# Two root-mean-square norms after the expert output: per-token sums in the expert stage, scaling, split, step-size product and store inside the second block's stage

## The reference, cut to what matters

```
x = x + mod[5][:, None, :] * peer(h, ...)        # first block, its end
x = rms_norm(x, final_g)                         # "final1": x * rsqrt(mean(x*x) + 1e-6) * final_g
h = rmsnorm(x, norm_w[l])                        # "norm_2", second block, its beginning
proj = h @ w_in[l]
a_q, a_f, a_i, a_z, b_x, b_z, c_z, c_xbc, c_dt, gate_logits = jnp.split(proj, split_idx, axis=-1)
...
x = x + jnp.sum(gates * branch_out, axis=2)      # the output of final1 is the residual
```

## Time and profile before

| | before |
|---|---|
| median of 3 runs | 4773.05 us |
| lowest and highest run | 4767.39, 4774.24 us |
| the profiled execution, its own time | 4772.02 us |
| its span | 4770.2 us |
| PE busy | 4418.3 us, 93% |
| DVE busy | 2832.7 us, 59% |
| ACT busy | 1814.2 us, 38% |
| POOL busy | 48.0 us, 1% |
| mean granted clock of PE | 0.965 |

### The profile page before, as it was taken

One profiled execution on the slowest core, in us unless ns is written; L12 is line 12 of the kernel. 1 busy time (PEld: TensorE's weight loads), 2 busy tenths in 40 slices (PEclk: granted clock), 3 DMA queues, 4 the chain that ended last, 5 costly groups with the idle time before them and its releaser, 6 DMA issues. The chain is left out here.

```text
span 4770.2 us, 76796 instructions
## 1 busy us (share of the span) xinstructions
PE 4418.3 (93%) x29238; PEld 3850.8 (81%) x29238; DVE 2832.7 (59%) x4753; ACT 1814.2 (38%) x2638; POOL 48.0 (1%) x63
## 2 busy tenths in 40 slices
PE   9798999897998995879999999999999599999996
PEld 1694444876998995879999999788888399999996
DVE  0448775665686446545776666455555556765645
ACT  0430000442653322334444555444444355444532
POOL 0000000000000000000000000000000000200000
PEclk9899999989999997989999999999999799999998
DMA  8357554326875331445665555666666255444452
GB/s 320 109 176 256 220 217 170 124 86 229 293 238 184 87 88 67 156 153 176 208 205 183 178 177 178 211 217 212 214 217 214 78 177 172 151 157 153 169 185 106
DMA packets 229517, 848.34 MB, mean 178 GB/s; under 512 B 86368, under 2 KB 124608, under 8 KB 139968
## 3 DMA queue, kind: packets, MB, share of 16 engines
q1 hardware_dynamic: 229312, 845.48, 52.0%
HBM read 794.95 MB, written 50.45 MB: 177 GB/s over the span
## 5 line engine op out<-in xcount | busy, mean ns | idle before, releaser
L282 DVE TENSOR_TENSOR rounded<-arena,rounded 128x1024 fp32r<-128x1024 f32 x464 | 567.7, 1225 | 647.1 <-ACT rounded L275 647.1
L275 ACT ACTIVATE rounded<-arena 128x1024 fp32r<-128x1024 f32 x464 | 490.6, 1059 | 787.0 <-PE bank L2340 391.3
L2018 PE MATMUL bank<-rounded,rounded 128*128 128x256 f32 x2048 | 590.8, 288 | 2.7 <-DVE rounded L2143 2.7
L2020 PE MATMUL bank<-rounded,rounded 128*128 128x256 f32 x2048 | 579.9, 283 | 0.0
L2019 PE MATMUL bank<-rounded,rounded 128*128 128x256 f32 x2048 | 579.7, 283 | 0.0
L351 PE MATMUL bank<-rounded,rounded 128*128 128x256 f32 x1664 | 479.1, 288 | 98.4 <-DVE rounded L282 98.4
L2701 PE MATMUL bank<-rounded,rounded 128*128 128x256 f32 x1856 | 533.4, 287 | 14.8 <-DVE rounded L2932 14.5
L2702 PE MATMUL bank<-rounded,rounded 128*128 128x256 f32 x1856 | 525.9, 283 | 0.0
L2703 PE MATMUL bank<-rounded,rounded 128*128 128x256 f32 x1856 | 525.8, 283 | 0.0
L352 PE MATMUL bank<-rounded,rounded 128*128 128x256 f32 x1664 | 477.9, 287 | 0.0
L353 PE MATMUL bank<-rounded,rounded 128*128 128x256 f32 x1664 | 477.3, 287 | 0.0
(11 more groups left out here) (383 smaller groups left out, 8807.6 us busy)
## 6 DMA issues: line engine op xcount, KB each, us to landing
arena<-in_w_in SPq DMA_DIRECT2D x244, 1024.0 KB, 4.9
arena<-in_peer_u SPq DMA_DIRECT2D x128, 1024.0 KB, 5.1
arena<-in_peer_v SPq DMA_DIRECT2D x128, 1024.0 KB, 4.8
arena<-in_w_mod SPq DMA_DIRECT2D x96, 1024.0 KB, 6.7
arena<-in_w_out SPq DMA_DIRECT2D x40, 1024.0 KB, 4.8
arena<-in_w_conv_out SPq DMA_DIRECT2D x16, 1024.0 KB, 4.9
arena<-in_w_dn_out SPq DMA_DIRECT2D x16, 1024.0 KB, 4.8
arena<-in_peer_w_q SPq DMA_DIRECT2D x16, 1024.0 KB, 4.8
```

The source lines that it names most:

```text
L275: act.activation(k.staged(0, b), k.raw(r % 2)[:, c], ACT.Copy).then_inc(k.hi_done, 1)
L282: dve.tensor_tensor(k.staged(1, q), k.raw(r % 2)[:, c], k.staged(0, q), ALU.subtract).then_inc(k.lo_done, 1)
L2018: pe.matmul(out, wh, hi(kt), start=(kt == 0), stop=False)
L2020: mm = pe.matmul(out, wl, hi(kt), start=False, stop=(kt == KT - 1))
```

## The change

In `expert_output` the sum goes to slots 80 to 95 (`total`). While DVE adds, ACT squares each slot, PE multiplies each square (as the stationary operand, 128 channels x 128 tokens) with two columns, ones and `final_g` squared, which gives both sums for each token in banks 6 and 7 (`sums`), and POOL writes `total * (final_g * norm_w)` to slots 48 to 63 (`scaled`). Transposes have banks 0 to 5 only.

The stages of both norms, `save`, `dt_product` and `split` are gone. At the start of `mixers` two roots, two reciprocals and a product are taken on tiles of 128 tokens x 2; four matmuls with the identity spread two rows of inverses over all partitions (`spread`); DVE scales slots 48 to 63 in four pieces of 128x1024 (`h_scaled`) and makes their low parts (`h_lower`) after ACT has made the high parts. PE waits for the piece that it needs in tile 0. `final`, 16 operations on DVE, two for each half i below 8, gives the residual in slots 80 to 95, and SP stores it ahead of the load of tile 8. `dt_product` is 48 rounded matmuls behind half 4.

```
 def expert_output(..., x_saved, following3, sum_slot, scaled_slot):
+        @block.gpsimd
+        def _(pool):
...
+            for m in range(KT):
+                pool.wait_ge(added, m + 1)
+                pool.tensor_tensor(scaled(m), total(m), both[:, m:m + 1].broadcast_to([P, L]), ALU.mult).then_inc(scaled_done, 1)
...
+            def sums(m):
...
+                pe.wait_ge(squared, m + 1)
+                for tt in range(2):
+                    mm = pe.matmul(k.ps[6 + tt][:, 0:2], square(m)[:, tt * P:(tt + 1) * P], ones_gains[:, m, :],
+                                   start=(m == 0), stop=(m == KT - 1))
+                mm.then_inc(square_read, 1)
...
-                if m >= 8:
-                    pe.wait_ge(added, m - 7)
+                if m >= 6:
+                    pe.wait_ge(added, m - 5)
...
                 mm.then_inc(turned, 1)
+                if m >= 4:
+                    sums(m - 4)
+            for m in range(KT - 4, KT):
+                sums(m)
...
+            for m in range(KT):
+                act.wait_ge(added, m + 1)
+                if m >= 4:
+                    act.wait_ge(square_read, m - 3)
+                act.activation(square(m), total(m), ACT.Square).then_inc(squared, 1)
...
 def mixers(k, w, hi, lo, following3, sum_slot, hi_slot, lo_slot, x_saved):
+            sp.dma_start(wdt, k.i["w_dt"]).then_inc(wdt_in, 16)
             for j in range(2, tiles):
+                if j == 8:
+                    sp.wait_ge(final_done, KT)
+                    sp.dma_start(x_saved, k.t(sum_slot, KT)).then_inc(x_out, 16)
...
+            pe.wait_ge(n_dve, 5)
+            spread(row12, inv12)
+            spread(row1, inv1)
...
+                    if j == 0 and kt % 4 == 0:
+                        pe.wait_ge(h_low, kt // 4 + 1)
...
+                if i == 4:
+                    dt_product()
...
+            for tt in range(2):
+                act.activation(root1[:, tt:tt + 1], k.ps[6 + tt][:, 0:1], ACT.Sqrt, bias=k.eps[:, 0:1], scale=1.0 / D).then_inc(n_act, 1)
+            high(0, 0)
+            act.wait_ge(n_dve, 3)
+            act.activation(root2, mean2, ACT.Sqrt, bias=k.eps[:, 0:1], scale=1.0 / D).then_inc(n_act, 1)
+            high(0, 1)
+            for c in range(4):
+                act.wait_ge(scaled, c + 1)
+                act.activation(k.r(hi_slot + 4 * c, 4), k.t(lo_slot + 4 * c, 4), ACT.Copy).then_inc(h_high, 1)
+            act.wait_ge(wdt_in, 16)
+            act.activation(wdt_hi, wdt, ACT.Copy).then_inc(wdt_high, 1)
...
+            low(0, 0)
+            dve.wait_ge(row_set, 1)
+            h_scaled(0)
+            h_scaled(1)
+            h_lower(0)
+            low(0, 1)
+            h_scaled(2)
+            h_lower(1)
+            h_scaled(3)
+            h_lower(2)
+            h_lower(3)
+            dve.wait_ge(wdt_high, 1)
+            dve.tensor_tensor(wdt_lo, wdt, wdt_hi, ALU.subtract).then_inc(wdt_low, 1)
             for i in range(halves):
-                low(i // 2, i % 2)
+                if i >= 2:
+                    low(i // 2, i % 2)
+                if i < 8:
+                    final(2 * i)
+                    final(2 * i + 1)
...
-        rms_norm(k, "final1", ...)
-        rms_norm(k, "norm_2", ...)
-        save(k, 32, x2_saved)
-        dt_product(k, 48)
-        split(k, "split_h3", 48, 32, 48, saves=2)
```

More of the change, by code:

```diff
@@ L2407, in _ @@
                 dve.wait_ge(turned, m + 1)
[L2408 removed]
+                dve.scalar_tensor_tensor(out=total(m), in0=k.ps[m % 6][:, 0:L],
                                          scalar=gate[:, m:m + 1], in1=x, op0=ALU.mult, op1=ALU.add).then_inc(added, 1)
@@ L2497, in mixers @@
     csq, crs = (lambda j: tile(148, j)), (lambda g: tile(196, g))
+    total = lambda m: tile(sum_slot, m)
+    root1, inv1, mean2, root2, inv2 = (k.gst[:, m, :] if m < 4 else k.mod_c[:, 0:2] for m in range(5))
+    inv12 = k.mod_c[:, 2:4]
+    wdt, wdt_hi, wdt_lo = flat(k.t(104, 1)), k.r(105, 1)[:, 0, :], k.r(106, 1)[:, 0, :]
+    row12, row1 = k.ps[6][:, L:2 * L], k.ps[7][:, L:2 * L]
     LEVEL = lambda l: 70 + 6 * l
@@ L2690, in c_sums, with spread, dt_product @@
                     mm.then_inc(csummed, 1)
+            def spread(dst, src):
+                for tt in range(2):
+                    mm = pe.matmul(dst[:, tt * P:(tt + 1) * P], src[:, tt:tt + 1].broadcast_to([P, P]), k.ident[:],
+                                   start=True, stop=True)
+                mm.then_inc(row_set, 1)
+            def dt_product():
+                pe.wait_ge(wdt_low, 1)
+                out = k.ps[4][0:SH, 0:L]
+                for kt in range(KT):
+                    at = slice(kt * SH, (kt + 1) * SH)
+                    pe.matmul(out, wdt_hi[:, at], hi(kt), start=(kt == 0), stop=False)
+                    pe.matmul(out, wdt_hi[:, at], lo(kt), start=False, stop=False)
+                    mm = pe.matmul(out, wdt_lo[:, at], hi(kt), start=False, stop=(kt == KT - 1))
+                mm.then_inc(dt_ready, 1)
+            pe.wait_ge(n_dve, 5)
+            spread(row12, inv12)
+            spread(row1, inv1)
             for i in range(halves):
@@ L3122, in low_part, with final, h_scaled @@
                 dve.tensor_tensor(k.r(OUT_LO[b] + 4 * c, 4), x, k.r(OUT_HI[b] + 4 * c, 4), ALU.subtract).then_inc(split_low, 1)
+            def final(m):
+                dve.wait_ge(row_set, 2)
+                dve.scalar_tensor_tensor(out=total(m), in0=total(m), scalar=k.col("final_g")[:, m:m + 1], in1=row1,
+                                         op0=ALU.mult, op1=ALU.mult).then_inc(final_done, 1)
+            def h_scaled(c):
+                x = k.t(lo_slot + 4 * c, 4)
+                dve.tensor_tensor(x, x, row12.unsqueeze(1).broadcast_to([P, 4, L]), ALU.mult).then_inc(scaled, 1)
@@ new lines, in h_lower @@
+            def h_lower(c):
+                dve.wait_ge(h_high, c + 1)
+                dve.tensor_tensor(k.r(lo_slot + 4 * c, 4), k.t(lo_slot + 4 * c, 4), k.r(hi_slot + 4 * c, 4),
+                                  ALU.subtract).then_inc(h_low, 1)
+            dve.wait_ge(n_act, 2)
+            dve.reciprocal(inv1, root1).then_inc(n_dve, 1)
+            dve.wait_ge(n_dve, 1)
+            for tt in range(2):
+                at = slice(tt, tt + 1)
+                dve.scalar_tensor_tensor(out=mean2[:, at], in0=k.ps[6 + tt][:, 1:2], scalar=inv1[:, at], in1=inv1[:, at],
+                                         op0=ALU.mult, op1=ALU.mult).then_inc(n_dve, 1)
```

44 lines of the change are left out of this document (33 added, 11 removed).

## The result

Before 4771.1 us (median of 4 runs, 4767.39 to 4774.24), after 4722.12 us (4 runs, 4721.07 to 4733.11): ratio 0.9903, 95% interval 0.9886 to 0.992. The profiled execution took 4721.25 us (span 4719.4). The time lies on the forecast, 4722.0, and in its range.

What follows compares the result with a forecast made beforehand. A serial chain through DVE, ACT, DMA and barriers bounds the changed stretch; elsewhere dense PE does. Terms -56.7 + 5.7 + 0.5 + 0.5 = -50.0 us from 4772.0 gave 4722, range 4713 to 4735.

Steps and rivals of the forecast that it cites:

- A to T: Expert stage from last expert matmul's end (A) to mixer stage's start (T): adds end at 3742.6, T at 3745.5.
- T to the start of half 2: Mixer stage's head, from its start to the second weight tile: 19.7 us, set by DVE's low part.
- A to half 2, against before: Last expert matmul's end to second weight tile: half 2 starts at 3765.2 instead of 3821.94, 56.7 us less.
- Exp's table load at i = 11: Mixer stage, ACT: a 1.28 us load makes half 12's high part late, 0.5 us more (0 to 1.3).
- tile 8 behind the store: Mixer stage, SP's queue: tile 8's load stalls behind the 2 MB store, 0.5 us more (0 to 4.2).
- The head of the mixer stage: Chain of ACT, DVE and PE after T: PE's first weight matmul at T + 9.6, half 2 at T + 19.7.
- part 1: Expert stage gets longer: PE needs 0.85 us for each m, adds wait for PE, stage ends 6.5 us later.
- The rival of a longer half clock: Mixer stage: PE starts with gaps, so halves 2 and 3 and part of `dt_product` run slower; 4730, chance 0.12.
- The lock-out with DVE: Expert stage: POOL and DVE block each other in the adds, POOL's step 1.16 us; 4728, chance 0.10.
- the slower case with 3.9 us a product: Expert stage: POOL's product with a spread column is slow, gain gone at 3.9 us; 4783 with 4.6, chance 0.02.
- cannot be passed: SP's queue: ring order keeps tile 8's load from overtaking the store, so the stall is 0.5 us or more.
- Finals at nothing: Mixer stage, DVE: twelve `final` after half 1, two in each half, cost nothing; without cover 4.8 us.

Runs made afterwards that it cites:

- again: The changed kernel run once more without an edit, against the kernel before: median 4725.0 us, ratio 0.9913 (0.99 to 0.9927).
- after: The changed kernel as first measured, against the kernel before: 4722.12 us, ratio 0.9903 (0.9886 to 0.992).
- half the rows: Changed kernel with squares and gain columns rounded, one PE row per sum instead of two; ratio to the kernel before 0.9891 (0.9876 to 0.9906).
- the sums last: Changed kernel with all sums behind all transposes, squares in 16 slots; ratio to the kernel before 0.9908 (0.9893 to 0.9923).
- five profiles: Changed kernel twice, and with one wait for all token pieces, the store in eighths, or later final multiplications; 4722.12, 4725.0, 4731.01, 4728.14, 4730.36 us.
- The eighths: Changed kernel with the 2 MB store cut into eight 256 KB pieces, one ahead of each load of tiles 7 to 14; 4728.14 us, one run.
- extra matmuls: Sixteen small constant matmuls around the spreads, added to the changed kernel with rounded sums, store in eighths, moved tables and later finals; 4714.17 us, one run.

## Why the prediction was right, and where it wasn't

| term | forecast | measured |
|---|---|---|
| A to T | 16.05 | 20.17 (again: 21.57) |
| T to PE's first weight matmul | 9.6 | 9.8 |
| T to the start of half 2 | 19.7 | 19.6 |
| A to half 2, against before | -56.7 | -52.7 |
| `dt_product` | +5.7 | +5.4 |
| Exp's table load at i = 11 | +0.5 | +0.7 |
| tile 8 behind the store | +0.5 (0 to 4.2) | +1.7 |
| everything later | 0 | +1.8 |
| sum | -50.0 | -43.1 |

- **The direction and the bound** were right: a serial chain between two dense parts was shortened, from 92.5 to 39.8 us at half 2. The head of the mixer stage, the longest working of the prediction, holds within 0.2 us at both points (tile 0 ends at T + 18.7, 0.7 earlier than worked out, because the half clock lasted 2.4 us into the second piece, to 3757.4, and not 4.4; DVE's queue sets half 2 all the same).
- **The step that failed is the price of PE's work for one m** in part 1: 0.85 us, 0.33 for two transposes and 4 x 0.129 for the sums, all read from rows at the full clock. The clock was 0.50 for most of the stage. At the full clock the price was even too high: the first sums of after start 0.69 and 0.62 us apart (3725.24, 3725.93, 3726.55). At the half clock it was 1.17, with 0.21 a row of `sums`, so the adds came every 1.17 us and T 4.1 us late. I had asked what the clock is where PE starts after a pause, and not what it would be under the work that the change adds. The rival of a longer half clock put it behind T, where the head was as forecast; it lay ahead of T. Three things carry this: half the rows give 5.2 us back at T; with the sums last the adds keep their 0.40 us while the clock is 1.00; and in five profiles of one and the same stage T follows the moment of the fall. What makes the clock fall is less clear. The order counts: with the sums between the transposes it fell 3.1 to 5.8 us after A in ten profiles, with all transposes first 8.7 and 9.8 us. That the rows of `sums` themselves bring the fall isn't shown, as in two of the ten it came before the first of them; a pause of PE for the first square may do it as well, and no run parts the two.
- **POOL** was over-priced (0.69 against 0.57 to 0.61), at no cost, as PE ended last. The lock-out with DVE, and the slower case with 3.9 us a product, are refuted by POOL's 9.18 us for 16 beside adds at full pace. By the Trainium skill (SBUF — State Buffer, Who interferes with whom) a DVE instruction with at most one SBUF input, outside the 2-port modes, does not contend with GpSimd. The trace agrees: the adds have one and a gain column, and neither side was slowed.
- **The store** was mis-sized: 1.7 instead of 0.5. I had cut the sum of the three full transfer times, 16.0 us, to about 12 by an overlap of fixed latencies, which no row showed. From the issue of tile 7's load (3792.63) to the data of tile 8 (3807.71) it took 15.1. Tile 8's load was issued at 3799.55, so it took 8.2 us where a load had taken 4.7. The eighths take the wait away. By the Trainium skill (DMA: Bandwidth & Descriptors, Queues, rings and completion order) descriptors are consumed in ring order, but a later one may finish its write before an earlier one, so the prediction's "cannot be passed" says more than that. In the trace the store, issued at 3793.00, had landed at 3805.3, before the load behind it.
- **Finals at nothing** was nearly right: twelve cost nothing, but the first four put `low` of half 2 behind PE by 0.86 us. The text had them at 0.2.
- **Table loads** took 1.28 each, as read from the trace.
- **Everything later** is +1.8: +1.9 from the start of the high part of one late half of the mixer stage (4544.95 before, 4492.27 after) to the end of the span (225.25 to 227.13), and little else. That part was 226.19 and 226.28 in the second runs of the two kernels, so the 1.9 lies within the scatter.
- **The total** came out to 0.1 us because an A that came 7.7 us sooner, within the scatter of runs, made up for the 7 us too much that was promised behind it. That is luck. The change's own 43 us would have given about 4729 on the base used: inside the range, 7 above the forecast.

## What to carry to other kernels

When a change puts small matmuls on TensorE in a stage that had been at full clock, price them at both clock levels; here that was the largest error of the sum. Measure a change between two events around it, one the end of untouched work, since this kernel scatters by 12 us ahead of the change. When a hole is closed, look at what each chain in it ends on: here rounding, two table loads, the size of one store and the place of four small steps were worth 12 us more.

## What the runs showed of the hardware

- Busy time of PE alone doesn't tell its clock. In the changed kernel the granted clock stayed at 0.50 with PE busy 4.00 of 4.00 us on transposes and rows with two moving columns (3734 to 3738). In the kernel before it was still 1.00 over a stretch with 0.66 us of transposes in 3 us. Twenty rows with 128 columns and the spreads behind them, begun at 0.50, were followed by 1.00 (extra matmuls).
- The moment at which the clock falls differs from run to run of one and the same stage: 3.3 to 5.6 us after A in five profiles, and T - A moved with it by 1.9 us.
- A float32 row with two moving columns took 0.11 us at the full clock (28 in 3.00 us) and 0.20 to 0.21 us at the half clock (25 in 5.00 us), about twice, as the clock.
- POOL's product of 128x256 with a column spread over its tokens takes 0.57 to 0.61 us, and doesn't disturb adds of DVE with one bank and one SBUF input and a column.
- A 2 MB store took 12.3 us to land with loads of 1 MB in the same queue, and 6.6 us alone; the loads' median in that stretch was 6.5, where it had been 4.7.
